# Mixer and gate weights split beside the quads of the feed-forwards and kept in DRAM; stores moved one quad later in the queue

## The chip, the cores and the metric

The kernel runs on one core of a Trainium2 chip. The metric is the device time of one execution in microseconds, lower is better. The core has a matrix engine (TensorE, PE in the profile, with its weight loads as PEld), VectorE (DVE), ScalarE (ACT), GpSimd (POOL), and SyncE (SP), which here only issues DMA transfers.

## The reference

One decoder layer on 1024 tokens of width 1024, in float32:

```
x = x + 0.5 * swiglu(rms_norm(x, ffn1_norm), ffn1_w_gu, ffn1_w_down)        # D_FF = 2816
q, k, v, u = split(rms_norm(x, mix_norm) @ w_in)                             # 512, 128, 128, 512
a = sliding_window_attention(rms_norm(q), rms_norm(k), v, rel_bias, sinks)   # window 128
m = multiscale_pool(u, pool_w, pool_scale)
x = x + concatenate([a, m]) @ w_out
x = x + 0.5 * swiglu(rms_norm(x, ffn2_norm), ffn2_w_gu, ffn2_w_down)
gate = sigmoid(rms_norm(x, ple_norm) @ ple_w_gate + ple_b_gate)
x = x + gate * rms_norm(p @ ple_w_proj, ple_post_norm)
```

## The kernel before, in words

Every large product is made of three matmuls: each float32 operand is split into a rounded part (hi, made by ScalarE) and the rest (lo, made by VectorE), and PE adds hi*hi, hi*lo and lo*hi in one bank (`three`, lines 859 to 863). Activations lie transposed, features on partitions, tokens in two halves of 512.

The program runs through six stages: the embedding projection (`e_tile`, 16 tiles copied through the buffers `et` to DRAM), the first feed-forward (phase 0), the token mixer, the second feed-forward (phase 1), and the gates.

A feed-forward is computed by a fast scheme of seven products instead of eight. Its gate and up weights come as 22 quads of 1 MB (`quad_load`). Quads 0 and 1 are computed directly (`first_product`), from quad 2 on each quad has seven products in the order P1, Q6, Q7, Q5, P2, Q4, Q3 (`product`), each of 12 matmuls. Their weight tiles live in a ring of TR = 12 slots; four of the seven are sums (`add_t`). VectorE combines the products (`quad`: w2, w3, c22, c21, c12), ScalarE copies P1 (`copy_p1`) and applies the silu to both halves (`gate0`, `gate1`). P2 adds onto P1's bank and so waits for the copy; Q3 adds onto Q5's bank and so waits for c22 (`wait_bank`, lines 948 and 963). VectorE then writes gated products (`gated`) and, after an odd quad, four mixed ones (`mix_acts`).

Beside the quads run, in SP's queue (`ffn`, lines 678 to 746): `act_store`, each second quad, of 1792 KB; for each of 22 chunks of the down weights a load (`wd_load`), four sums on POOL (`down_weights`), and a store (`wd_store`), both in the quad of the load (`wd_chunk`); and in phase 0 one piece of the embedding per quad (`e_piece`), which ScalarE squares and VectorE adds, with the sum stored after eight pieces (`e_parts`, which waits for the landing), and at quad 4 the band of relative biases. SP issues in program order and a wait holds all behind it. Then come the 77 steps of the down products (`down`), with a ring of six slots.

The mixer works through a list of steps, `PLAN`. Its weights come as 36 units of 512 KB (w_in and w_out, each column of tiles for both token halves), the gates' as 16. Each is loaded into one of two buffers raw_m, rounded by ScalarE and split by VectorE (`round_unit`, `split_unit`) into one of four slots, three units ahead of its use; the first four of a stage and the pooling weights are split during the down products. On both engines the split stands in front of what the step itself asks of them:

```
if kind in ("win", "wout") and SLOTS <= MIXU_AT[step] + LATE:
    m = MIXU_AT[step] + LATE
    if m < N_MIXU:
        split_unit(U_MIX + m)
```

Of the kernel before, what the change touches and what calls it, by code (L numbers as in the profile page):

```python
# [13 lines left out]
P = 128  # L14
# [44 lines left out]
NRAW = 2  # L59
# [6 lines left out]

LATE = SLOTS - 1
# [24 lines left out]
TR = 12  # L92
# [16 lines left out]
WD_TWO = (6, 10, 14, 17)  # L109
WD_TURN, _at = {}, 0  # L110
for _q in range(2, QUADS):
    _n = min(2 if _q in WD_TWO else 1, N_WD - _at)
    WD_TURN[_q] = tuple(range(_at, _at + _n))
    _at += _n
# [20 lines left out]
T_GAP = 1  # L135

# [66 lines left out]
def dram_unit(what, i):  # L203
# [18 lines left out]
UNIT_STEPS = [{FH + 7 + 4 * i: n for i, n in enumerate(range(U_POOLW, U_MIX + SLOTS))},  # L222
              {FH + 7 + 4 * i: n for i, n in enumerate(range(U_GATE, U_GATE + SLOTS))}]
# [38 lines left out]
def program(nc, xT, pT, units, gu, wd, poolw, small, const, onehot, rel, band_row, band, e_dram, actc, wdc, x1, out):  # L262
    with ExitStack() as ctx:
# [76 lines left out]
        raw_m = [place(f"raw_m{i}", (P, UNIT), cb + 32 * KB + 4 * KB * i) for i in range(NRAW)]  # L340
# [9 lines left out]
        def t_slot(n):  # L350
            return (n + 6) % TR
# [3 lines left out]
        t_hi = [place(f"t_hi{i}", (P, 4 * P), t_at(i) + 2 * KB, F32R) for i in range(TR)]  # L355
        ring_at = [r2, r2 + 8 * KB, t_at(10), t_at(0), t_at(2), t_at(4)]
# [104 lines left out]
        raw_in = [sem(f"raw_in{i}") for i in range(NRAW)]  # L461
        unit_hi, unit_split = sem("unit_hi"), sem("unit_split")
# [8 lines left out]
        e_out = [sem(f"e_out{i}") for i in range(4)]  # L471
# [127 lines left out]
        def _(sp):  # L599
            def unit_load(n):  # L600
                src, size = (poolw, NG * P) if n == U_POOLW else (units[mix_unit(n)], UNIT)
                if n >= NRAW:
                    sp.wait_ge(unit_split, n - NRAW + 1)
                sp.dma_start(raw_m[n % NRAW][:, 0:size], src).then_inc(raw_in[n % NRAW], 16)

# [56 lines left out]
            def e_piece(n):  # L662

                a, d = n // KT, n % KT
                if n == 0:
                    for i in range(4):
                        sp.wait_ge(e_out[i], 16 * (2 * KT // 4))
                    sp.wait_ge(s_made, made(0, "h", 1, KT - 1))
                elif d > 1:
                    sp.wait_ge(e_added, a * (KT - 1) + d - 1)  # L670
                sp.dma_start(e_part[d > 0][:, :], e_dram[a, :, d, :]).then_inc(e_back, 16)

            def e_parts(a):
                sp.wait_ge(e_added, (a + 1) * (KT - 1))
                sp.dma_start(e_dram[a, :, KT, :], e_part[0][:, :]).then_inc(e_parted, 16)
                sp.wait_ge(e_parted, 16 * (a + 1))

            def ffn(ph, first_units):
# [3 lines left out]
                for q in range(1, QUADS):  # L682
# [16 lines left out]
                    for c in WD_TURN.get(q, ()):  # L699
# [1379 lines left out]
```

## Time and profile before

| what | value |
|---|---|
| median of 3 runs | 1738.04 us (1737.92 to 1738.63) |
| the profiled execution's own time | 1737.11 us |
| its span, first to last instruction | 1735.3 us |
| mean granted TensorE clock | 0.992 |
| PE busy | 1684.5 us, 97% of the span |
| VectorE busy | 1255.8 us, 72% |
| ScalarE busy | 698.6 us, 40% |
| GpSimd busy | 233.7 us, 13% |
| DMA | 282.95 MB, mean 163 GB/s |

Busy time is the time in which an engine runs an instruction. The granted clock is a share of TensorE's full 2.4 GHz; 0.50 in a window means the lower level, 1.2 GHz, throughout it. In a timeline a row gives start and duration in us, engine, source line, operation, the tensors out<-in, and in brackets the idle time just before it and what ended it. Where the quads run, phase 0 covers about 90 to 490 us of the span, the mixer about 690 to 1005 and phase 1 from there on; the gates are the last 90 us.

### The profile page before, as it was taken

The numbers are of one execution on the slowest core, as the hardware profiler recorded it, in microseconds if no ns is written. First come the engines' busy times: TensorE is split into PE (matmuls) and PEld (weight loads), VectorE is DVE, ScalarE is ACT, GpSimd is POOL, SyncE is SP. The second block draws the span as 40 slices with busy tenths as digits, with TensorE's granted clock in tenths as the row PEclk, the third lists the DMA queues.
The fourth block names the chain that finished last, engine by engine and source line by source line (L and its number), as shares of the span: only waits on it lengthen the run. The fifth ranks groups of instructions, "written<-read, shape, count | busy, mean of one in ns | idle before, by whom it ended". The sixth has DMA issues, their size and how long they took to land.

```text
span 1735.3 us, 20459 instructions
## 1 busy us (share of the span) xinstructions
PE 1684.5 (97%) x7348; PEld 1371.6 (79%) x7348; DVE 1255.8 (72%) x1794; ACT 698.6 (40%) x1121; POOL 233.7 (13%) x245
## 2 busy tenths in 40 slices
PE   6999999999899999999999999999999999999998
PEld 4878877888788888776677788888888888888877
DVE  6888686767756768687877788777667755676785
ACT  5533232322345444356655443232223234534442
POOL 0012222222100000044140001221212300000000
PEclk9999999999999999999999999999999999999999
DMA  8135554554579765121123213454445439876533
GB/s 292 55 140 188 176 194 174 214 176 176 176 239 317 218 193 161 61 63 58 42 66 121 87 64 128 176 189 169 169 159 188 164 128 302 273 243 190 167 105 121
DMA packets 127784, 282.95 MB, mean 163 GB/s; under 512 B 10523, under 2 KB 52164, under 8 KB 119364
## 3 DMA queue, kind: packets, MB, share of 16 engines
q1 hardware_dynamic: 124376, 275.57, 47.4%
q10 hardware_dynamic: 3308, 6.08, 0.9%
q8 instruction: 59, 0.97, 0.2%
q14 instruction: 41, 0.34, 0.1%
HBM read 204.52 MB, written 78.66 MB: 163 GB/s over the span
## 4 chain that ended last, share of the span: by engine, by line
PE 61%; DMA 15%; DVE 13%; POOL 5%; ACT 4%; issue 3%; SPq 0%; ACTq 0%; DVEq 0%; POOLq 0%
PE bank L861 20%; PE bank L862 19%; PE bank L863 19%; DMA wdr<-in_wd 9%; POOL wdr L843 5%; DMA wdc<-wdr 3%; DVE qb L1902 1%; DVE hn L1521 1%; PE bank L1107 1%; ACT probs L1445 1%; DVE w_lo L1736 1%; DVE probs L1914 1%; DVE dn_lo L1728 1%; DMA e_dram<-et 1%; DMA e_dram<-e_acc 1%
## 5 line engine op out<-in xcount | busy, mean ns | idle before, releaser
L861 PE MATMUL bank<-h_hi,t_hi 128*128 128x512 f32 x704 | 274.9, 390 | 0.5 <-ACT p L1239 0.5
L862 PE MATMUL bank<-h_lo,t_hi 128*128 128x512 f32 x704 | 273.9, 389 | 0.0
L863 PE MATMUL bank<-h_hi,t_lo 128*128 128x512 f32 x704 | 273.9, 389 | 0.0
L843 POOL TENSOR_TENSOR wdr<-wdr 128x256 f32<-128x256 f32 x176 | 168.7, 959 | 748.0 <-DMA wdr<-in_wd 737.6
L1728 DVE TENSOR_TENSOR dn_lo<-d_f,dn_hi 128x1024 fp32r<-128x1024 f32 x154 | 185.1, 1221 | 116.0 <-ACT dn_hi L1256 115.7
L861 PE MATMUL bank<-dn_hi 128*128 128x512 f32 x616 | 241.1, 391 | 0.6 <-DVE dn_lo L1728 0.6
L862 PE MATMUL bank<-dn_lo,dn_hi 128*128 128x512 f32 x616 | 239.7, 389 | 0.0
L863 PE MATMUL bank<-dn_hi,dn_lo 128*128 128x512 f32 x616 | 239.7, 389 | 0.0
L861 PE MATMUL bank<-c_hi,t_hi 128*128 128x512 f32 x544 | 213.0, 392 | 10.4 <-DVE c L1600 9.0
L1256 ACT ACTIVATE dn_hi<-d_f 128x1024 fp32r<-128x1024 f32 x154 | 159.9, 1056 | 151.7 <-DMA d_f<-in_wd 78.2
L862 PE MATMUL bank<-c_lo,t_hi 128*128 128x512 f32 x544 | 212.2, 390 | 0.0
L863 PE MATMUL bank<-c_hi,t_lo 128*128 128x512 f32 x544 | 212.2, 390 | 0.0
L861 PE MATMUL bank<-h_hi,w_hi 128*128 128x512 f32 x416 | 172.1, 414 | 6.8 <-ACT sig L1485 2.6
L862 PE MATMUL bank<-h_lo,w_hi 128*128 128x512 f32 x416 | 164.0, 394 | 0.0
L863 PE MATMUL bank<-h_hi,w_lo 128*128 128x512 f32 x416 | 163.7, 394 | 0.0
L1221 ACT ACTIVATE t_hi<-t_f 128x512 fp32r<-128x512 f32 x160 | 96.0, 624 | 152.5 <-DVE t_f L1564 145.7
L861 PEld LDWEIGHTS bank<-h_hi,t_hi 128*128 128x128 f32 x704 | 132.2, 188 | 29.4 <-issue 1.4
L862 PEld LDWEIGHTS bank<-h_lo,t_hi 128*128 128x128 f32 x704 | 132.2, 188 | 27.7 <-issue 0.5
L863 PEld LDWEIGHTS bank<-h_hi,t_lo 128*128 128x128 f32 x704 | 132.2, 188 | 27.5
L861 PEld LDWEIGHTS bank<-dn_hi 128*128 128x128 f32 x616 | 115.6, 188 | 26.0 <-DVE dn_lo L1728 1.5
L862 PEld LDWEIGHTS bank<-dn_lo,dn_hi 128*128 128x128 f32 x616 | 115.7, 188 | 24.6 <-issue 0.7
L863 PEld LDWEIGHTS bank<-dn_hi,dn_lo 128*128 128x128 f32 x616 | 115.6, 188 | 24.2
(163 smaller groups left out, 2491.2 us busy)
## 6 DMA issues: line engine op xcount, KB each, us to landing
raw<-in_gu SPq DMA_DIRECT2D x44, 1024.0 KB, 6.0
d_f<-actc SPq DMA_DIRECT2D x154, 256.0 KB, 3.2
actc<-acts SPq DMA_DIRECT2D x20, 1792.0 KB, 7.8
raw_m<-in_units SPq DMA_DIRECT2D x52, 512.0 KB, 4.1
wdr<-in_wd SPq DMA_DIRECT2D x44, 512.0 KB, 5.4
wdc<-wdr SPq DMA_DIRECT2D x44, 512.0 KB, 3.4
d_f<-wdc SPq DMA_DIRECT2D x88, 256.0 KB, 3.2
d_f<-in_wd SPq DMA_DIRECT2D x66, 256.0 KB, 4.4
```

The source lines that it names most:

```text
L843: pool.tensor_tensor(blocks[to], blocks[one], blocks[two], ALU.add).then_inc(wd_made, 1)
L861: pe.matmul(ps, whi, vhi, start=first, stop=False, skip_group_check=onto)
L862: pe.matmul(ps, whi, vlo, start=False, stop=False, skip_group_check=onto)
L863: return pe.matmul(ps, wlo, vhi, start=False, stop=last, skip_group_check=onto)
L1107: last = pe.matmul(score_bank[h // 2][:, c + off:c + 2 * P], q_sb[p0:p0 + HEAD_DIM, h, b * P:(b + 1) * P], k_sb[p0:p0 + HEAD_DIM, max(b - ...
L1221: act.activation(t_hi[i][:, :], src, ACT.Copy).then_inc(t_rounded, 1)
L1256: act.activation(dn_hi[slot][:, :], d_f[slot][:, :], ACT.Copy).then_inc(dn_rounded, 1)
L1445: last = act.activation(probs[:, h, off:], probs[:, h, off:], ACT.Exp, bias=stats[:, NEGM, h:h + 1], accum_out=stats[:, DEN, h:h + 1])
L1521: dve.scalar_tensor_tensor(hn[k % 2][:, :], x_sb[:, k, tok(nrm % 2)], col(g), rstd[nrm % 2][:, :], ALU.mult, ALU.mult).then_inc(h_normed, 1)
L1728: dve.tensor_tensor(dn_lo[slot][:, :], d_f[slot][:, :], plain(dn_hi[slot][:, :]), ALU.subtract).then_inc(dn_split, 1)
L1736: dve.tensor_tensor(lo, raw_m[n % NRAW][:, 0:size], plain(hi), ALU.subtract).then_inc(unit_split, 1)
L1902: link(dve.reciprocal(qb[j % 2][:, :], qb[j % 2][:, :]))
```

## The change

The units are split once each, not once for each token half: 10 of w_in, 8 of w_out (phase 0, quads 2 to 19) and 8 of the gate (phase 1, quads 2 to 9). Each quad loads one unit, rounds and splits it, and stores both parts to a new DRAM tensor hl (26 units of 1 MB) one quad later. The mixer and the gates load the finished parts, two DMAs of 512 KB for each of the 52 uses, straight into the four slots; ScalarE and VectorE no longer touch them. The unit's buffers take two slots of the tile ring, so TR is 10. In SP's queue the stores of tiles, sums and units stand one quad after their loads. The head copies with eight et buffers and in another order, the first norm's sum stands after tile 4 instead of 2, and quad 3's first sums move ahead of quad 2.

```
-WD_TWO = (6, 10, 14, 17)
+WD_TWO = (7, 13)
-for _q in range(2, QUADS):
+for _q in range(1, QUADS - 1):
...
-TR = 12
+TR = 10
+NET = 8
+U_QUAD = 2
+N_SPLIT = N_IN + 2 * KT
+SPLITS = [list(range(N_IN + KT)), list(range(N_IN + KT, N_SPLIT))]
...
+        def unit_ready(n):
+            return w_in[(n - U_MIX) % SLOTS], 32 * ((n - U_MIX) // SLOTS + 1)
...
             def unit_load(n):
...
+                if slot_free(n):
+                    sp.wait_ge(main_made, slot_free(n))
+                else:
+                    sp.wait_ge(gu_made, NGU if n < U_GATE else 2 * NGU)
+                    sp.wait_ge(unit_out, 32 * (len(SPLITS[0]) if n < U_GATE else N_SPLIT))
+                s = (n - U_MIX) % SLOTS
+                sp.dma_start(plain(w_hi[s][:, :]), hl[mix_unit(n) - W_IN][:, 0:UNIT]).then_inc(w_in[s], 16)
+                sp.dma_start(plain(w_lo[s][:, :]), hl[mix_unit(n) - W_IN][:, UNIT:2 * UNIT]).then_inc(w_in[s], 16)
+
+            def split_load(u):
+                if u:
+                    sp.wait_ge(unit_out, 32 * u)
+                sp.dma_start(unit_f[:, :], units[W_IN + u]).then_inc(unit_in, 16)
+
+            def split_store(u):
+                sp.wait_ge(unit_lo, u + 1)
+                sp.dma_start(hl[u][:, 0:UNIT], plain(unit_rounded[:, :])).then_inc(unit_out, 16)
+                sp.dma_start(hl[u][:, UNIT:2 * UNIT], plain(unit_low[:, :])).then_inc(unit_out, 16)
...
             def e_parts(a):
...
-                sp.wait_ge(e_parted, 16 * (a + 1))
...
-                    if ph == 0 and 0 <= q - E_QUAD <= 2 * KT:
-                        n = q - E_QUAD
-                        if n and n % KT == 0:
-                            e_parts(n // KT - 1)
-                        if n < 2 * KT:
-                            e_piece(n)
+                    if 0 < q - U_QUAD <= len(SPLITS[ph]):
+                        split_store(SPLITS[ph][q - U_QUAD - 1])
                     if q % 2 == 0:
                         act_store(ph, q // 2 - 1)
+                    if q - 1 in WD_TURN:
+                        wd_store(ph, WD_TURN[q - 1][-1])
+                    n = q - E_QUAD
+                    if ph == 0 and n in (KT, 2 * KT):
+                        e_parts(n // KT - 1)
+                    if q in WD_TURN:
+                        wd_load(ph, WD_TURN[q][0])
+                    if ph == 0 and 0 <= n < 2 * KT:
+                        e_piece(n)
+                    if 0 <= q - U_QUAD < len(SPLITS[ph]):
+                        split_load(SPLITS[ph][q - U_QUAD])
                     if ph == 0 and q == BAND_QUAD:
...
-                    for c in WD_TURN.get(q, ()):
-                        wd_chunk(ph, c)
...
                         quad_load(ph, q + 3)
+                    for a, b in zip(WD_TURN.get(q, ()), WD_TURN.get(q, ())[1:]):
+                        wd_store(ph, a)
+                        wd_load(ph, b)
...
                     gate0(ph, q)
-                    gate1(ph, q)
                     if ph == 0 and 0 <= q - E_QUAD < 2 * KT:
                         e_squares(q - E_QUAD)
+                    if 0 <= q - U_QUAD < len(SPLITS[ph]):
+                        round_unit(SPLITS[ph][q - U_QUAD])
+                    gate1(ph, q)
...
                 make_c21(ph, q)
+                if ph == 0 and 0 <= q - E_QUAD < 2 * KT:
+                    e_accumulate(q - E_QUAD)
+                if 0 <= q - U_QUAD < len(SPLITS[ph]):
+                    split_unit(SPLITS[ph][q - U_QUAD])
                 make_c12(ph, q)
...
-                if kind in ("win", "wout") and SLOTS <= MIXU_AT[step] + LATE:
-                    m = MIXU_AT[step] + LATE
-                    if m < N_MIXU:
-                        round_unit(U_MIX + m)
...
             round_pj(0)
-            round_pj(1)
             act.wait_ge(small_in, 16)
-            for k in range(KH):
-                x_square(0, k)
             for n in range(2 * KT):
                 e_tile(n)
-                if n < 2:
...
+                if n == 0:
+                    x_square(0, 0)
+                    x_square(0, 1)
+                    round_pj(1)
+                elif n < 4:
+                    x_square(0, 2 * n)
+                    x_square(0, 2 * n + 1)
+                elif n == 4:
                     std(0)
```

## Rows read from the trace of the kernel before

**Rows 1.** PE's waits: who ended them, us in total, times, longest.

```profile
PE bank L861 <- DVE pj_lo L1849: 9.4, 1, 9.4
PE bank L861 <- DVE c L1600: 9.0, 5, 5.0
PE bank L861 <- DVE probsT_lo L1875: 6.6, 3, 4.3
PE bank L1118 <- DVE probs L1927: 6.3, 5, 2.4
PE bank L861 <- ACT et L1360: 4.7, 3, 2.6
PE bank L861 <- ACT sig L1485: 2.6, 2, 1.3
PE bank L861 <- DVE h_lo L1527: 2.6, 1, 2.6
```

**Rows 2.** Windows: us, busy (instructions) of PE, PEld, DVE, ACT, POOL, PEclk, DMA share, GB/s.

```profile
440.00:444.00 4.00, 4.00 (x12) 3.14 (x12) 2.57 (x5) 0.63 (x1) 0.00 (x0) 0.63 0.93 360
764.00:768.00 4.00, 4.00 (x14) 2.93 (x14) 1.92 (x2) 1.96 (x4) 0.00 (x0) 0.60 0.51 152
824.00:828.00 4.00, 4.00 (x8) 2.12 (x7) 2.87 (x12) 0.80 (x4) 0.00 (x0) 0.50 0.12 50
957.00:961.00 4.00, 3.65 (x11) 2.88 (x12) 1.15 (x3) 1.49 (x2) 0.00 (x0) 0.67 0.11 40
```

**Rows 3.** Timeline of ACT and PE around quads 2 and 3, both phases.

```profile
1069.60 0.60 ACT L1239 ACTIVATE p<-bank 128x512 f32<-128x512 f32 x1 [3.40 <-PE bank L863]
...
1088.64 0.60 ACT L1239 ACTIVATE p<-bank 128x512 f32<-128x512 f32 x1 [4.08 <-PE bank L863]
...
104.76 0.47 PE L861 MATMUL bank<-c_hi,t_hi 128*128 128x512 f32 x1 [1.41 <-DVE t_lo L1576]
```

**Rows 4.** Chain of waits (start, us, what), phase 0, and SP's timeline, phase 1.

```profile
107.58 7.60 DMA wdr<-in_wd
...
119.88 3.40 DMA wdc<-wdr
...
123.30 6.53 DMA wdr<-in_wd
...
137.72 18.46 DMA wdr<-in_wd
...
1062.55 0.33 SPq L625 DMA_DIRECT2D actc<-acts  x1
```

**Rows 5.** Splits of units and VectorE's mixed sums: by tile, by form, timeline.

```profile
L1736 DVE TENSOR_TENSOR w_lo<-raw_m,w_hi x52: 1207/1220/2078, 535.8 to 1711.1; 128x1024 fp32r<-128x1024 f32 x52
...
L1263 ACT ACTIVATE w_hi<-raw_m 128x1024 fp32r<-128x1024 f32 x28 | 29.3, 1046 | 4.2 <-DMA raw_m<-in_units 4.2
...
104.57 2.61 DVE L1643 TENSOR_TENSOR acts<-acts 128x512 f32<-128x512 f32 x4
```

**Rows 6.** Timeline of ACT and PE in phase 0.

```profile
213.06 0.63 ACT L1231 ACTIVATE e_part<-e_part 128x512 f32<-128x512 f32 x1 [11.45 <-DMA e_part<-e_dram]
...
222.22 0.47 PE L861 MATMUL bank<-c_hi,t_hi 128*128 128x512 f32 x1 [2.20 <-DVE c L1600]
...
439.71 0.77 PE L861 MATMUL bank<-c_hi,t_hi 128*128 128x512 f32 x1 [5.05 <-DVE c L1600]
```

**Rows 7.** Timeline of PE and ACT in the mixer.

```profile
764.00 0.79 PE L861 MATMUL bank<-h_hi,w_hi 128*128 128x512 f32 x1 [2.57 <-DVE h_lo L1527]
...
820.48 1.09 PE L1118 MATMUL bank<-const_sb,probs 128*128 128x128 f32 x8 [2.40 <-DVE probs L1927]
...
957.35 0.50 PE L861 MATMUL bank<-probsT_hi,v_hi 128*128 128x512 f32 x1 [4.29 <-DVE probsT_lo L1875]
...
950.96 1.06 ACT L1263 ACTIVATE w_hi<-raw_m 128x1024 fp32r<-128x1024 f32 x1 [4.25 <-DMA raw_m<-in_units]
```

**Rows 8.** Timeline of PE at the first feed-forward product.

```profile
42.30 0.50 PE L861 MATMUL bank<-h_hi,t_hi 128*128 128x512 f32 x1
```

More of the change, by code:

```diff
@@ L58 @@
 W_GATE = W_OUT + KT
-NRAW = 2
 N_MIXU = 2 * N_IN + 2 * KT
@@ L218 @@
 assert N_WIN0 % 2 == 0 and N_GATE0 % 2 == 0
-UNIT_STEPS = [{FH + 7 + 4 * i: n for i, n in enumerate(range(U_POOLW, U_MIX + SLOTS))},
-              {FH + 7 + 4 * i: n for i, n in enumerate(range(U_GATE, U_GATE + SLOTS))}]
+POOLW_STEP = FH + 7
+U_QUAD = 2
+N_SPLIT = N_IN + 2 * KT
+SPLITS = [list(range(N_IN + KT)), list(range(N_IN + KT, N_SPLIT))]
 def unit_of(step):
@@ L259, with program @@
 H_AT = {2: 0, 3: 1, 6: 2, 7: 3}
-def program(nc, xT, pT, units, gu, wd, poolw, small, const, onehot, rel, band_row, band, e_dram, actc, wdc, x1, out):
+def program(nc, xT, pT, units, gu, wd, poolw, small, const, onehot, rel, band_row, band, hl, e_dram, actc, wdc, x1, out):
     with ExitStack() as ctx:
@@ L339, in program @@
         w_lo = [place(f"w_lo{i}", (P, UNIT), cb + 8 * KB * i + 4 * KB, F32R) for i in range(SLOTS)]
-        raw_m = [place(f"raw_m{i}", (P, UNIT), cb + 32 * KB + 4 * KB * i) for i in range(NRAW)]
+        raw_m = place("raw_m", (P, NG * P), cb + 32 * KB)
         sq = [place(f"sq{i}", (P, HALF), cb + 40 * KB + 2 * KB * i) for i in (0, 1)]
@@ L355, in program @@
         t_hi = [place(f"t_hi{i}", (P, 4 * P), t_at(i) + 2 * KB, F32R) for i in range(TR)]
+        unit_f = place("unit_f", (P, UNIT), t_at(TR + 1))
+        unit_rounded = place("unit_rounded", (P, UNIT), t_at(TR), F32R)
+        unit_low = place("unit_low", (P, UNIT), t_at(TR + 1), F32R)
         ring_at = [r2, r2 + 8 * KB, t_at(10), t_at(0), t_at(2), t_at(4)]
@@ L398, in program @@
         pj_lo = [place(f"pj_lo{i}", (P, UNIT), t_at(t_slot(FIRST + i)), F32R) for i in (0, 1)]
-        et = [place(f"et{i}", (P, HALF), cb + 2 * KB * i) for i in range(4)]
+        et = [place(f"et{i}", (P, HALF), cb + 2 * KB * i) for i in range(NET)]
         gband = place("gband", (N_Q_HEADS, SKEW), cb + 24 * KB)
-        oh_sb = place("oh_sb", (N_BUCKETS + 1, SKEW), t_at(t_slot(FIRST + 2)))
+        oh_sb = place("oh_sb", (N_BUCKETS + 1, SKEW), t_at(TR))
         e_part = [place("e_acc", (P, HALF), acc_at[1]), place("e_part", (P, HALF), rstd_at[1])]
@@ L460, in program @@
         x1_out = [sem(f"x1_out{a}") for a in (0, 1)]
-        raw_in = [sem(f"raw_in{i}") for i in range(NRAW)]
-        unit_hi, unit_split = sem("unit_hi"), sem("unit_split")
+        poolw_in, poolw_hi, poolw_split = sem("poolw_in"), sem("poolw_hi"), sem("poolw_split")
+        unit_in, unit_hi, unit_lo, unit_out = sem("unit_in"), sem("unit_hi"), sem("unit_lo"), sem("unit_out")
+        w_in = [sem(f"w_in{i}") for i in range(SLOTS)]
         pj_in, pj_rounded, pj_split = [sem(f"pj_in{i}") for i in (0, 1)], sem("pj_rounded"), sem("pj_split")
@@ L470, in program @@
         e_copied = sem("e_copied")
-        e_out = [sem(f"e_out{i}") for i in range(4)]
+        e_out = [sem(f"e_out{i}") for i in range(NET)]
         re_out = [sem(f"re_out{a}") for a in (0, 1)]
@@ L665, in e_piece @@
                 if n == 0:
-                    for i in range(4):
-                        sp.wait_ge(e_out[i], 16 * (2 * KT // 4))
+                    for i in range(NET):
+                        sp.wait_ge(e_out[i], 16 * (2 * KT // NET))
                     sp.wait_ge(s_made, made(0, "h", 1, KT - 1))
+                elif d == 0:
+                    sp.wait_ge(e_parted, 16)
                 elif d > 1:
@@ L737, in ffn @@
                         else:
-                            for j in range(4):
-                                sp.wait_ge(e_out[j], 16 * (2 * KT // 4))
+                            for j in range(NET):
+                                sp.wait_ge(e_out[j], 16 * (2 * KT // NET))
                             for a in (0, 1):
@@ L1198, in round_s @@
                     act.wait_ge(gu_made, ph * NGU + FIRST)
-                elif what == ("s", Q5, 0) and ph == 0:
-                    for i in range(4):
-                        act.wait_ge(e_out[i], 16 * (2 * KT // 4))
+                elif what == ("h", 1, 0) and ph == 0:
+                    for i in range(NET):
+                        act.wait_ge(e_out[i], 16 * (2 * KT // NET))
                 act.activation(operand("hi", what), source(what), ACT.Copy).then_inc(s_rounded, 1)
@@ L1693, in quad @@
                 todo = [(q + 1, s) for s in LOS1] if more else []
-                if ph == 0 and 0 <= q - E_QUAD - 1 < 2 * KT:
-                    e_accumulate(q - E_QUAD - 1)
                 if q == 2:
                     split_t(ph, *todo[0])
-                if more:
+                elif more:
                     add_t(ph, q + 1, 0)
@@ L1708, in quad @@
                 make_w3(ph, q)
-                for x in todo[1:3]:
+                for x in todo[1 + (q == 2):3]:
                     split_t(ph, *x)
@@ L1991, in build @@
     x1 = nc.dram_tensor("x1", (D_MODEL, SEQ), F32, kind="Internal").ap()
-    program(nc, xT, pT, units, gu, wd, poolw, small, const, onehot, rel, band_row, band, e_dram, actc, wdc, x1, out)
+    program(nc, xT, pT, units, gu, wd, poolw, small, const, onehot, rel, band_row, band, hl, e_dram, actc, wdc, x1, out)
 def constants():
```

115 lines of the change are left out of this document (52 added, 63 removed).

## The prediction

> **What bounds the kernel now.** Read first the shares of the page: PE is busy 1684.5 of 1735.3 us, and no matmul is added or taken away, so the change can only move PE's 50.8 us of idle time and the time at the lower clock. The list of PE's waits splits the idle time [rows 1]: 9.4 us before the first matmul, 4.7 for the copies of the embedding tiles (et), 9.0 for the sums of the quads (c), 15.5 in the mixer (probsT_lo, probs, h_lo), 2.6 in the gates (sig). The windows [rows 2] show what a gap costs beyond itself: after gaps of over 2.3 us the clock stood at 0.50 to 0.67, the lower of the two levels for most of 4 us, so 1.3 to 2.0 us of work lost each; behind 824:828 a part of the windows before is lost as well, and over the whole mixer I count 8.2 us so, from its windows' clock. The gap before 439.71 [rows 6] cost another 1.5 to 1.7.
>
> **The clock of a quad.** p1 is copied at 1069.60 and 1088.64 [rows 3]: a quad takes 19.04 us, one of its seven products 2.72. In its order P1, Q6, Q7, Q5, P2, Q4, Q3, the product P2 starts 10.9 us into the quad and needs the p1 copy; Q3 starts at 16.3 and needs c22. VectorE's instructions on 128x512 follow each other every 0.65 us (2.61 for four, [rows 5]). A split on 128x1024 is 1.05 on ScalarE and 1.22 on VectorE, at worst 2.08 [rows 5]; I take 1.05 and 1.3.
>
> **What the queue now carries.** Each split stands before gate1 on ScalarE and before c12 on VectorE. If the unit is not there, everything behind waits: gate1 and the next quad's p1 copy on ScalarE; c12, two gated products, (after an odd quad) four mixed ones, the next quad's four sums, splits, w2, w3 and c22 on VectorE. From the end of the split to that c22 are 13 instructions (8.5 us), 17 (11.1 us) after an odd quad. So PE stalls once a split ends later than 7.8 us (even quad) or 5.2 us (odd) into the next quad. The load of the unit is issued last: behind the store of the unit before (two transfers of 512 KB), the store of the sums (1792 KB, each second quad), the store of the tiles, and the tiles' load, which waits until that store has landed. Price of these waits [rows 4]: sums and a 512 KB tile issued together land after 7.60 us from the second issue, 8.0 from the first; a lone 512 KB store takes 3.40, a load with others before it 6.53. I take 6.1 for tiles, embedding piece and unit together (1280 KB; between 3.4 and 7.6 by the rows), and 6.2 for unit store plus tile store.
> - Odd quad, split to split: 6.2 + 6.1 + 1.05 + 1.3 + some 1 us of issue and overlap with POOL = 15.7.
> - Even quad: 4.7 (c12, gated, mixed) + 8.0 + 6.1 + 2.35 + 1 = 22.2.
> Together 37.9 against 38.1 for PE's two quads: just balanced, an odd quad recovers what an even one loses. In this steady part I cost the change at 0 to 2 us; the cover is gone once a pair of quads needs more (rival below).
>
> The Trainium skill, GPSIMD Engine Reference, section Specifications, says that GpSimd and VectorE share their SBUF interfaces when a VectorE instruction has two inputs there. The split's 2.08 beside its 1.22 [rows 5] agrees; 26 splits that all met the tile sums would take 22 us more of VectorE. The Trainium skill, DMA: Bandwidth & Descriptors, section Anatomy of one DMA, gives about 2.0 us plus bytes over 436 GB/s: 5.0 us for the 1280 KB where I took 6.1, and 7.4 where the trace has 8.0; by it the two first-unit stalls below would each be 1 us shorter.
>
> **Part by part.**
> 1. *First unit, phase 0.* In quad 2 nothing has been fetched ahead. The store of the sums is issued 0.4 us before 107.58 [rows 4]; the tile store, now ready by then, takes the place of the load that landed 7.60 later: about 116.3 with 1 us for VectorE slowed by the tile sums. Then 6.1: 122.4. Split done 124.7, c22 of quad 3 at 133.2. Quad 2's last product starts at 104.76 [rows 3], so quad 3 at 107.48 and its Q3 at 123.8: a stall of 9.4, of which 6.3 fall already at P2 (copy ready 124.7, wanted 118.4). I take 8.5, since parts of VectorE's chain overlap, plus 1.5 of clock: +10. Bounds +5 to +13.
> 2. *Phase 1, the same place.* VectorE and SP run as in phase 0, shifted by 955.3 (1062.55 against 107.2, [rows 4]); PE's quad 3 starts at 1066.9 [rows 3], shifted by 959.4. So 4.1 us more cover, and no embedding piece (0.8): stall 3.5 to 4.5, clock 1: +5. Bounds 0 to +8.
> 3. *The band* is sent at quad 4 behind the unit. In 137.72's row [rows 4] a tile waited 18.46 us behind sums, weights and band; at the 2304 KB per 8.0 us of the pair about 11 of it are the others, 8 the band. It now delays quad 5's unit store, so its split ends some 10.5 us into quad 6: 5.3 over the limit, with clock +6. Bounds 0 to +10.
> 4. *Two tiles in quads 7 and 13.* The second one's sums are stored only in the next quad, behind POOL (4.6 us of sums between 115.26 and 119.88, [rows 4]) and before the tile load: lag 10.5 against 7.8, twice: +5. Bounds 0 to +8.
> 5. *What goes.* SP no longer waits within a quad for POOL, nor for the embedding sum's landing. That wait held ScalarE 11.45 us at 213.06 and PE 2.20 at 222.22, and 5.05 at 439.71 [rows 6]. All of c's 9.0, 0.5 for the copy, 1.7 clock: -11. Bounds -4 to -11. Late next are the units of 1, 3 and 4.
> 6. *Head.* Eight et buffers and the copies ahead of the squares take away the 4.7 us for et [rows 1] and the slow clock behind it. The first norm now stands after tile 4, behind all eight squares, and gives back about 2, as the reciprocal comes 1 us later. The first gate product, now at 42.30 [rows 8], starts 3 us sooner: -3. Bounds 0 to -6.
> 7. *Mixer.* 28 splits leave each of both engines between 726 and 1006: 29.3 us of ScalarE and 28 times 1.22 or more of VectorE [rows 5]. The gap at 764.00 (2.57) ends VectorE's alternating of norm tiles and splits; the one at 957.35 (4.29) follows a ScalarE wait of 4.25 for a unit queued behind the next phase's weights [rows 7]. Both lose 2.5 to 3. Before 820.48 a split stands ahead of the scores: 1.2 of 2.40 [rows 7]. In sum I count 13 of the 15.5 plus 1.5 for smaller waits as going, 6.5 of the 8.2 of clock, and 3 coming back since PE catches up with the reciprocals: -17. Bounds -6 and -23. A slot's 1 MB has three units of 24 matmuls (16 us) to arrive, 8.0 us by the pair: 0.
> 8. *Gates:* 12 splits less; sig's 2.6 [rows 1] mostly goes: -2. Bounds 0 to -3.
> 9. *Ten t slots for twelve, reordered sums of quad 3, fewer splits in the down products:* 0; the fourth sum now waits for Q7, for which w3 behind it waits anyway, and PE shows no wait in the down products. Uncovered, the slots would cost one product, 2.7.
>
> Sum: 10 + 5 + 6 + 5 - 11 - 3 - 17 - 2 = -7, against this execution's 1737.1 us: 1730. The median of the runs shown is 0.9 higher; I say 1731.
>
> **Rivals.**
> - *The SP round trip becomes the bound (slower).* If DMA under the added 1.5 MB per quad, or POOL beside VectorE, makes a pair of quads take 40.5 instead of 37.9, each pair from quad 4 on costs 2.4: seven pairs 17, and 4 of clock. It decides from 38.1 on, 0.2 above my sum. For it: the tile behind mixed traffic took 6.53 although its bytes alone need half. Against: the pair landed 2304 KB in 8.0 us, 288 KB per us, and by the sizes of the transfers two quads now carry about 9.3 MB in 38 us, 245 KB per us. Time 1731 + 21 = 1752, with half the drift 1742.
> - *The stalls 1 to 4 hardly show,* as VectorE and the products have more slack than I read; then only 5 to 8 act with a third of the 26: 1738 - 33 + 9 = 1714. For it: phase 1 before has no quad stall. Against: the 5.05 at 439.71 shows that late sums do reach PE.
> - *The mixer's gaps are the chain scores, exp, probs itself,* and removed splits only turn into VectorE idle time: gain 7 instead of 17: 1741. For it: probs alone holds 6.3 us of PE's waits [rows 1]. Against: 957.35.
>
> **Chances.** My sum 0.40 (own range 1724 to 1738), SP bound 0.27, no stalls 0.18, mixer chain 0.15. About 0.2%, 3.5 us, is what a measurement here tells from no change. Faster: 0.30 of the first, all of the third: and 0.03 of the rest, 0.51. Same: 0.07 of the first, 0.05 of the second, 0.06 of the last: 0.18. Slower: the rest, 0.31. The range runs from near the stall-free case to most of the SP case: 1714 to 1752.
>
> **What would show it.** PE waits for p1 or c at quad 3 of both phases, ScalarE's split there waiting for DMA over 8 us; another at quads 6, 8 and 14; no PE wait over 3 us in the mixer; clock near 1.0 there. Wrong would be a first-unit stall under 4 us, or waits for c in every second quad.

## The result, and the profile after

The changed kernel takes 1716.28 us (median of 3 runs, 1715.31 to 1719.83) against 1738.04: ratio 0.9879, 95% interval 0.9856 to 0.9901. The prediction was 1731, range 1714 to 1752: 7 us faster forecast, 21.8 measured. The direction and the range held, the size did not: 1716.3 lies at the fast end of the range of 1714 to 1752, and outside the 1724 to 1738 that the prediction gave its own sum.

Each profiled execution is cut at PE's first matmul of each kind of work; the lengths of the stages show where the time went (us):

| stage | before | after | difference | predicted |
|---|---|---|---|---|
| head, to the first gate product | 42.30 | 40.97 | -1.3 | -3 |
| quads, phase 0 | 439.85 | 442.58 | +2.7 | +10 (parts 1, 3, 4, 5) |
| down products, phase 0 | 212.89 | 212.71 | -0.2 | 0 |
| mixer | 308.17 | 281.29 | -26.9 | -17 |
| quads, phase 1 | 425.23 | 432.37 | +7.1 | +5 |
| down products, phase 1 | 210.83 | 210.81 | 0.0 | 0 |
| gates | 96.03 | 92.77 | -3.3 | -2 |

PE's waits after (who ended them, us in total, times, longest), to be laid beside [rows 1]:

```profile
PE bank L889 <- ACT p L1268: 10.2, 2, 6.4
...
PE bank L889 <- DVE c L1629: 4.3, 3, 1.9
PE bank L917 <- DVE acc L1538: 2.0, 1, 2.0
PE bank L889 <- ACT et L1392: 1.6, 2, 1.0
...
PE bank L1146 <- DVE probs L1961: 1.0, 1, 1.0
```

probsT_lo, h_lo and sig are gone from the list, probs fell from 6.3 to 1.0, c from 9.0 to 4.3. New is p, ScalarE's copy of P1, with 10.2 in two waits; both stand in quad 3, behind the first unit of a phase. The gap before acc, 2.0 where it was 0.7, is what the head gives back.

The five new or remaining gaps of the quads after, besides the 1.4 of quad 2 that was there before (timeline of PE; start, duration, in brackets the idle time before it and what ended it):

```profile
123.66 0.77 PE L889 MATMUL bank<-h_hi,t_hi 128*128 128x512 f32 x1 [6.40 <-ACT p L1268]
...
191.18 0.47 PE L889 MATMUL bank<-c_hi,t_hi 128*128 128x512 f32 x1 [1.65 <-DVE c L1629]
...
250.65 0.47 PE L889 MATMUL bank<-c_hi,t_hi 128*128 128x512 f32 x1 [1.89 <-DVE c L1629]
...
365.95 0.47 PE L889 MATMUL bank<-c_hi,t_hi 128*128 128x512 f32 x1 [0.78 <-DVE c L1629]
...
1055.89 0.77 PE L889 MATMUL bank<-h_hi,t_hi 128*128 128x512 f32 x1 [3.83 <-ACT p L1268]
```

How the first comes about is read from SP's timeline and then ScalarE's, the counterpart of [rows 4]:

```profile
107.71 0.33 SPq L647 DMA_DIRECT2D actc<-acts  x1
108.08 0.59 SPq L643 DMA_DIRECT2D wdc<-wdr  x1
114.77 0.58 SPq L639 DMA_DIRECT2D wdr<-in_wd  x1
115.67 0.33 SPq L693 DMA_DIRECT2D e_acc<-e_dram  x1
116.05 0.42 SPq L621 DMA_DIRECT2D unit_f<-in_units  x1
...
119.50 0.63 ACT L1260 ACTIVATE e_acc<-e_acc 128x512 f32<-128x512 f32 x1 [15.90 <-DMA e_acc<-e_dram]
121.45 1.06 ACT L1289 ACTIVATE unit_rounded<-unit_f 128x1024 fp32r<-128x1024 f32 x1 [1.33 <-DMA unit_f<-in_units]
122.42 0.61 ACT L1277 ACTIVATE w<-w 128x512 f32<-128x512 f32 x1
122.94 0.58 ACT L1268 ACTIVATE p<-bank 128x512 f32<-128x512 f32 x1
```

SP stands from 108.7 to 114.8 for the tile store to land; only then does it issue the tile, the embedding piece and the unit. ScalarE waits 15.90 us for the piece, then 1.33 more for the unit, and the copy of p, which has to wait behind both and behind gate1, comes 6.4 us late for PE.

The clock behind the two long gaps (windows of 4 us; us, busy time and instructions of PE, PEld, DVE, ACT and POOL, granted clock, DMA share, GB/s):

```profile
124.00:128.00 4.00, 4.00 (x10) 3.10 (x10) 3.78 (x7) 0.66 (x2) 0.00 (x0) 0.50 0.85 335
128.00:132.00 4.00, 4.00 (x15) 3.01 (x13) 4.00 (x8) 3.20 (x6) 0.00 (x0) 0.78 0.49 154
...
1056.00:1060.00 4.00, 4.00 (x10) 3.17 (x11) 3.78 (x8) 0.77 (x2) 0.59 (x1) 0.50 0.79 313
1060.00:1064.00 4.00, 4.00 (x16) 3.10 (x14) 4.00 (x8) 3.33 (x7) 0.00 (x0) 0.80 0.52 159
...
192.00:196.00 4.00, 4.00 (x19) 3.31 (x18) 2.04 (x4) 0.00 (x0) 0.00 (x0) 1.00 0.65 189
```

Two windows at 0.50 and 0.78 are 2.0 + 0.9 us of work lost, at 0.50 and 0.80 2.0 + 0.8. In this profile the clock stays at 1.00 behind the gap of 1.65 at 191.18, and behind 1.89 and 0.78 too. Such costs do not repeat from one execution to the next, as the last section shows.

The mixer as one window, before and then after:

```profile
695.00:1003.20 308.20, 290.98 (x1259) 226.99 (x1259) 232.49 (x438) 159.28 (x326) 64.80 (x65) 0.97 0.24 75
```

```profile
696.30:977.50 281.20, 279.94 (x1259) 222.93 (x1258) 192.93 (x406) 129.82 (x294) 58.66 (x65) 1.00 0.44 145
```

The same 1259 matmuls: PE's idle time falls from 17.2 to 1.3 us, its busy time from 291.0 to 279.9, by 11.0. The granted clock explains 8.4 of the 11.0: so much do PE's busy time and the missing share of the clock give, multiplied and summed over windows of 0.5 us, and after the change the clock is 1.00 throughout. The other 2.6 are matmuls that took longer at a granted clock of 1.00. VectorE is busy 39.6 us less, ScalarE 29.5 less.

### The profile page after: what moved, and what is told of

Its sections match the earlier page's. It is cut to its first block and busy times, and to the rows that moved or that the text cites. A ratio compares the mean times of both kernels' runs of the same rounds, so it can differ in the third digit from the quotient of the medians.

```text
span 1713.5 us, 20509 instructions
## 1 busy us (share of the span) xinstructions
PE 1678.1 (98%) x7348; PEld 1371.2 (80%) x7348; DVE 1196.9 (70%) x1768; ACT 677.1 (40%) x1095; POOL 227.2 (13%) x245
## 5 line engine op out<-in xcount | busy, mean ns | idle before, releaser
L889 PE MATMUL bank<-h_hi,t_hi 128*128 128x512 f32 x704 | 277.0, 393 | 10.2 <-ACT p L1268 10.2
L1763 DVE TENSOR_TENSOR dn_lo<-d_f,dn_hi 128x1024 fp32r<-128x1024 f32 x154 | 184.9, 1220 | 125.0 <-ACT dn_hi L1285 124.7
L889 PEld LDWEIGHTS bank<-h_hi,t_hi 128*128 128x128 f32 x704 | 133.2, 189 | 39.9 <-issue 11.5
```

Source lines behind the costliest of these rows:

```text
L889: pe.matmul(ps, whi, vhi, start=first, stop=False, skip_group_check=onto)
L1763: dve.tensor_tensor(dn_lo[slot][:, :], d_f[slot][:, :], plain(dn_hi[slot][:, :]), ALU.subtract).then_inc(dn_split, 1)
```

## The experiments

The kernel before was timed anew beside each group of runs, and its median was 1738.6 to 1740.9 there; so ratios are compared rather than medians. The stage lengths are those of the profiled executions. Where the code of a stage is the same they repeat to 0.1 us in the mixer and to 2 us in the quads of phase 0. Theory A and rival B are those of the expectation that stands above each reading.

| run | median | ratio, 95% interval | quads 0 | mixer | quads 1 |
|---|---|---|---|---|---|
| changed kernel | 1716.28 | 0.9879 (0.9856 to 0.9901) | 442.58 | 281.29 | 432.37 |
| e1_early | 1712.26 | 0.984 (0.9821 to 0.9859) | 441.66 | 281.32 | 430.49 |
| e2_unit_first | 1698.11 | 0.9757 (0.9741 to 0.9773) | 433.80 | 281.36 | 426.96 |
| e9_two_early | 1693.26 | 0.9737 (0.9719 to 0.9754) | 427.88 | 281.38 | 425.22 |
| e12_tile_first | 1702.38 | 0.9786 (0.9773 to 0.9798) | 435.52 | 281.39 | 425.23 |
| e5_queue_only | 1731.79 | 0.9951 (0.9937 to 0.9965) | 430.20 | 309.39 | 425.23 |
| e7_band1 | 1714.95 | 0.9854 (0.9841 to 0.9868) | 442.49 | 281.39 | 432.67 |
| e11_two_moved | 1720.69 | 0.989 (0.9872 to 0.9909) | 446.64 | 281.33 | 432.66 |
| e6_heavier | 1725.2 | 0.9916 (0.9904 to 0.9929) | 449.43 | 281.38 | 432.64 |
| e8_net4 | 1716.76 | 0.9867 (0.9854 to 0.9879) | 443.25 | 281.39 | 432.53 |
| e3_mix_dve | 1732.32 | 0.9961 (0.9947 to 0.9974) | 441.82 | 297.38 | 432.11 |
| e4_mix_act | 1718.08 | 0.9878 (0.9857 to 0.99) | 442.14 | 283.72 | 432.89 |
| e10_mix_both | 1736.64 | 0.9989 (0.9977 to 1.0001) | 443.61 | 302.49 | 432.33 |

### The mixer: e3_mix_dve, e4_mix_act, e10_mix_both

e3 adds this to VectorE's loop over the steps of the mixer:

```
             for step in PLAN:
                 kind = step[0]
+                if kind in ("win", "wout") and SLOTS <= MIXU_AT[step] + 3 < N_MIXU:
...
+                    dve.tensor_tensor(pad_d[:, :], pad_d[:, :], pad_d[:, :], ALU.subtract).then_inc(pad_dve, 1)
```

e4 adds the same to ScalarE's loop, with a copy, and e10 adds both:

```
+                    act.activation(pad_a[:, :], pad_a[:, :], ACT.Copy).then_inc(pad_act, 1)
```

> The changed kernel with 28 padding subtractions on 128x1024 put back on VectorE in the mixer, at the steps where the splits of the kernel before stood (in place on an unused region; they wait for nothing else). It computes the same. Theory A (VectorE's time was what held PE in the mixer, 13 of the 15.5 us of waits through VectorE): most of the 26.9 us that the mixer gained is given back, 15 to 20: 1732 to 1736, with PE waits for probs, h_lo and probsT_lo as in the kernel before. Rival B (the splits held PE by what they waited for, the rounding on ScalarE and a unit behind other transfers, not by their time): under 6 us: 1722 or less.

> The changed kernel with 28 padding copies on 128x1024 put back on ScalarE in the mixer, at the steps where the roundings stood, VectorE without its padding. It computes the same. Theory A: ScalarE was busy for half of the mixer only (159 of 308 us), so its 29.3 us cost PE little: 0 to 5 us, 1716 to 1721. Rival B (ScalarE holds probsT and the copies at the end of the chain of scores, exp, probs): 8 us or more, 1724.

> The changed kernel with both paddings. Theory A: the engines' time is nearly all: the sum of the two alone plus 1 to 3 us, 20 us or more over the changed kernel, about 1737; what is then missing of 26.9 is what the late unit at 957.35 cost (4.3 of wait and its 2 of clock). Rival B: far under 20 us; the rest, over 10 us, was waiting for data, not engine time.

The list has 32 such steps, not 28: the row with 28 in [rows 5] begins at 726, and four stand before it. VectorE's padding alone, 233.5 - 192.9 = 40.6 us of its time, gives back 16.1 us of the mixer's 26.9, and 0.8% of the 1.2% by the ratios. ScalarE's padding alone lengthens the mixer by 2.4 us, which does not show in the ratio. Both together give back 21.2 us, and the gain as a whole is gone but for 0.1% (the interval reaches 1.0001). Theory A holds in all three. Of the 2.6 us of longer matmuls at full clock 2.0 are back under e3, which adds nothing but VectorE's work; so they go with the waits for VectorE, though how is not shown. PE's gaps under e3 (timeline of PE):

```profile
781.04 0.66 PE L1149 MATMUL bank<-const_sb,probs 128*128 128x128 f32 x4 [1.82 <-DVE probs L1972]
817.50 1.09 PE L1149 MATMUL bank<-const_sb,probs 128*128 128x128 f32 x8 [2.40 <-DVE probs L1972]
...
947.92 0.50 PE L892 MATMUL bank<-probsT_hi,v_hi 128*128 128x512 f32 x1 [0.45 <-DVE probsT_lo L1916]
```

The 2.40 is the gap of 820.48 in [rows 7], now with a subtraction that waits for nothing: VectorE's time makes it. The gap of 957.35 in [rows 7] (4.29) comes back only as 0.45. The padding waits for no unit, so that gap was the late unit; with the slow clock behind it (957:961 at 0.67, [rows 2]) it is 3.8 + 1.3 = 5.1 of the 5.7 us that both paddings leave open (308.2 - 302.5).

### The first units: e1_early

```
                     if q + 3 < QUADS:
                         ...
                         quad_load(ph, q + 3)
+                    if q == 1:
+                        if ph == 0:
+                            e_piece(0)
+                        split_load(SPLITS[ph][0])
```

(both left out in quad 2)

> The changed kernel, with the first unit of each phase (and the first embedding piece) loaded one quad earlier, at quad 1, where the DMA queues stand idle. Theory A (the first unit's load, queued behind the sums and the first tile, is the whole of the wait at quad 3): the waits 6.40 (phase 0) and 3.83 (phase 1) for p go, and with them 2.9 and 2.8 us of slow clock: 1716.3 - 15.9 = 1700.4. Rival B (SyncE's chain of loads and stores is bound by itself, the first unit only sets where it starts): what goes at quad 3 comes back as waits for c in the quads behind, over 5 us of them per phase; 1708 or more.

Rival B, in the main. Both waits at quad 3 are gone, but phase 0's quads are only 0.9 us shorter and phase 1's 1.9. The waits for c behind them come to 8.3 us in phase 0; in phase 1 there is one of 3.37, less than the 5 that B named. The time, 1712.3, is B's. Timeline of PE under e1:

```profile
137.86 0.47 PE L893 MATMUL bank<-h_hi,t_hi 128*128 128x512 f32 x1 [2.21 <-ACT p L1272]
148.93 0.76 PE L893 MATMUL bank<-c_hi,t_hi 128*128 128x512 f32 x1 [5.35 <-DVE c L1633]
191.10 0.47 PE L893 MATMUL bank<-c_hi,t_hi 128*128 128x512 f32 x1 [1.24 <-DVE c L1633]
250.37 0.47 PE L893 MATMUL bank<-c_hi,t_hi 128*128 128x512 f32 x1 [1.73 <-DVE c L1633]
```

And the reason, from SP's timeline of the same run:

```profile
107.50 0.59 SPq L643 DMA_DIRECT2D wdc<-wdr  x1
114.17 0.57 SPq L639 DMA_DIRECT2D wdr<-in_wd  x1
...
115.44 0.43 SPq L625 DMA_DIRECT2D hl<-unit_rounded  x1
...
122.75 0.55 SPq L643 DMA_DIRECT2D wdc<-wdr  x1
128.43 0.57 SPq L639 DMA_DIRECT2D wdr<-in_wd  x1
...
129.69 0.43 SPq L621 DMA_DIRECT2D unit_f<-in_units  x1
```

The first unit was split by 111.2, but its store stood behind SP's wait for the tile store and went at 115.44, and the next unit's load behind the next tile store at 129.69. The lateness belongs to SP's row of waits, not to one transfer.

### The order in the queue: e2_unit_first, e9_two_early, e12_tile_first

e2 is e1 with the tile's load moved behind embedding piece and unit in every quad:

```
-                    if q in WD_TURN:
-                        wd_load(ph, WD_TURN[q][0])
                     if ph == 0 and 0 < n < 2 * KT:
                         e_piece(n)
                     if 0 < q - U_QUAD < len(SPLITS[ph]):
                         split_load(SPLITS[ph][q - U_QUAD])
+                    if q in WD_TURN:
+                        wd_load(ph, WD_TURN[q][0])
```

> As e1_early, and in every quad the embedding piece and the unit are sent ahead of the wait for the tile store, the tile behind them. Theory A (what is left of the waits for c in phase 0, 4.3 us at 191, 251 and 366, is the unit coming behind the tile): they go too, 1700.4 - 5 = 1695. Rival B (they come from VectorE's own load of work in those quads, or from POOL's sums, which now come later): the same as e1_early within 2 us, or up to 4 us more, with new waits behind POOL.

Theory A, and more than it said: ratio 0.9757, 14 us below e1 where 5 were expected. The waits at 191 and 250 are gone, and those behind the second unit shrank too, from 2.21 and 5.35 to 3.98 in phase 0 and from 3.37 to 1.45 in phase 1. One gap of 3.98 at 145.17 is left in phase 0 and 1.45 at 1069.10 in phase 1. e9 sends unit 0's store within quad 2 and unit 1's load at the end of it:

```
+                    if q == U_QUAD:
+                        split_store(SPLITS[ph][0])
                     if q in WD_TURN:
                         wd_load(ph, WD_TURN[q][0])
                     ...
-                    if q == 1:
+                    if q in (1, 2):
                         if ph == 0:
-                            e_piece(0)
-                        split_load(SPLITS[ph][0])
+                            e_piece(q - 1)
+                        split_load(SPLITS[ph][q - 1])
```

> As e2_unit_first; besides, unit 0 is stored within quad 2, ahead of that quad's tile load, and unit 1 (in phase 0 the second embedding piece too) is loaded at the end of quad 2 instead of in quad 3. Theory A (the wait of 3.98 for c at 145.17 and of 1.45 in phase 1 are the second unit, whose load at 124.61 waited for a store issued 4 us after the split had ended): both go, with some 2 us of clock: 1698 - 7 = 1691. Rival B (the lateness moves to the next quad again, as it did from quad 3 to quad 4 when the first unit came early): 1696 or more, with a wait for c at quad 5.

Theory A: 1693.26 us, ratio 0.9737, the best kernel here, 1.4% below the changed one. Its interval (0.9719 to 0.9754) overlaps that of e2 (0.9741 to 0.9773); the trace decides, since both of e2's waits are gone from it. Phase 1's quads are back at the length they have with no unit to split (425.22 against 425.23). All that PE still waits for in the quads of both phases, from its list of waits:

```profile
PE bank L895 <- DVE t_lo L1611: 1.4, 1, 1.4
...
PE bank L895 <- DVE c L1635: 0.6, 1, 0.6
```

The 1.4 was there before (1.41 at 104.76, [rows 3]). e12 keeps e9's start and puts the tile ahead of the unit again from quad 3 on.

> As e9_two_early (units 0 and 1 fetched ahead), but from quad 3 on the tile goes ahead of the embedding piece and the unit again, as in the changed kernel. Theory A (the prediction's balance of the loop, 37.9 us for a pair of quads against PE's 38.1, holds; only the start, the band and the two doubled tiles make it late): at most three waits for c, near quads 6, 9 and 15, 2 to 5 us in all; 1693 + 4 = 1697. Rival B (a loop with the tile ahead of the unit is too slow by itself): waits for c in every second quad, over 10 us; 1704 or more.

Between the two. By the waits it is A: two for c, in quads 6 and 15, 5.3 us in all, and none in phase 1, so the loop as changed does not drift. By the time, 1702.4, it is nearer to B's 1704 than to A's 1697. The wait behind the band is 4.28, with 2.8 of clock (0.50 and 0.76 in the two windows of 4 us from 184 on), where e9 has 0.57, so the order is worth 9 us here, more than the 4 expected. Timeline of PE under e12:

```profile
184.41 0.77 PE L895 MATMUL bank<-c_hi,t_hi 128*128 128x512 f32 x1 [4.28 <-DVE c L1635]
359.63 0.47 PE L895 MATMUL bank<-c_hi,t_hi 128*128 128x512 f32 x1 [1.00 <-DVE c L1635]
```

### The terms of the loop: e7_band1, e11_two_moved, e6_heavier

`BAND_QUAD = 4` becomes 1; `WD_TWO = (7, 13)` becomes `(10, 16)`; and for e6, with 48 in place of 32 in the waits for `unit_out`:

```
                 sp.dma_start(hl[u][:, UNIT:2 * UNIT], plain(unit_low[:, :])).then_inc(unit_out, 16)
+                sp.dma_start(more[u], plain(unit_low[:, :])).then_inc(unit_out, 16)
```

> The changed kernel with the band sent at quad 1 instead of quad 4. Theory A (part 3 of the prediction: the band delays the units behind it): the wait of 1.65 us for c at 191.18 goes, 1714.5. Rival B (that wait is what is left of the late first unit, which takes until quad 6 to be caught up): it stays at 1 us or more; 1716. A band that delays the first tile or the first unit instead would show as a longer wait than 6.40 at quad 3: 1718 or more.

The gap at 191.18 went, as A says, but so did those at 250.65 and 365.95, and in their place stands one wait of 11.76 at quad 3 (and 1.32 after it):

```profile
129.11 0.77 PE L889 MATMUL bank<-h_hi,t_hi 128*128 128x512 f32 x1 [11.76 <-ACT p L1268]
137.59 0.47 PE L889 MATMUL bank<-c_hi,t_hi 128*128 128x512 f32 x1 [1.32 <-DVE c L1629]
```

The longer wait at quad 3 is what the expectation named as a band that delays the first tile or unit, though not at its 1718 us: the time is 1714.95, and the stage is as long as in the changed kernel, 442.49 against 442.58. In quad 3 the waits are 6.7 us longer and the clock costs 1.4 us less (windows of 0.5 us: 1.6 against 3.0); that took the place of 4.3 us of waits in quads 6, 9 and 15. The likely reading is that once PE has been set back far enough, later delays of the queue fit into what it has lost already: the waits of one queue are not a sum of terms, PE pays for the latest point. It rests on this run and on e1.

> The changed kernel with the doubled tiles in quads 10 and 16 instead of 7 and 13. Theory A (part 4 of the prediction: the second tile delays the next unit): the waits for c at 250.65 (1.89) and 365.95 (0.78) go from there and stand three quads later, near 308 and 423; 1716 as before. Rival B (they are what was left of the late start): they stay at 250 and 366, 1716 too.

Theory A: the two gaps now stand three quads later. The time did not stay at 1716: the median is 1720.7 and the quads of phase 0 take 4.1 us more, though the ratios' intervals overlap. Of this 2.3 us are the gap at 427.37, which is 3.11 where the one at 365.95 was 0.78; the rest lies about as far as such runs differ.

```profile
309.72 0.47 PE L889 MATMUL bank<-c_hi,t_hi 128*128 128x512 f32 x1 [1.11 <-DVE c L1629]
...
427.37 0.47 PE L889 MATMUL bank<-c_hi,t_hi 128*128 128x512 f32 x1 [3.11 <-DVE c L1629]
```

> The changed kernel with a third store of 512 KB for every unit (the low half once more, to a place of its own that nothing reads), for which the next load waits as for the other two. Theory A (the loop has 0.2 us to spare for a pair of quads, so nearly every us that is added to it reaches PE): at the 288 KB per us of the prediction 1.8 us per quad, 3.4 per pair after the spare; eight pairs of phase 0 and three of phase 1: 30 to 40 us, 1746 to 1756. Rival B (the loop has more slack than reckoned, or the third store lies beside the others): under 10 us, 1726 or less.

Rival B: 0.4% over the changed kernel by the ratios, 9 us by the medians, 7 by the quads of phase 0 and 0.3 in phase 1. The waits for c still stand in quads 3, 6, 9 and 15 and not in every second quad (0.48, 4.45, 2.19 and 0.66). How much room there was is read from ScalarE's roundings of the units of quads 4, 5, 7, 8, 9, 10 and 11, first after (timeline of ScalarE):

```profile
156.65 1.06 ACT L1289 ACTIVATE unit_rounded<-unit_f 128x1024 fp32r<-128x1024 f32 x1 [1.27 <-DMA unit_f<-in_units]
177.91 1.06 ACT L1289 ACTIVATE unit_rounded<-unit_f 128x1024 fp32r<-128x1024 f32 x1 [2.00 <-DMA unit_f<-in_units]
...
213.79 1.06 ACT L1289 ACTIVATE unit_rounded<-unit_f 128x1024 fp32r<-128x1024 f32 x1 [0.86 <-DMA unit_f<-in_units]
239.97 1.06 ACT L1289 ACTIVATE unit_rounded<-unit_f 128x1024 fp32r<-128x1024 f32 x1 [1.54 <-DMA unit_f<-in_units]
255.81 1.06 ACT L1289 ACTIVATE unit_rounded<-unit_f 128x1024 fp32r<-128x1024 f32 x1 [1.14 <-DMA unit_f<-in_units]
277.34 1.06 ACT L1289 ACTIVATE unit_rounded<-unit_f 128x1024 fp32r<-128x1024 f32 x1 [2.00 <-DMA unit_f<-in_units]
291.20 1.06 ACT L1289 ACTIVATE unit_rounded<-unit_f 128x1024 fp32r<-128x1024 f32 x1 [0.79 <-DMA unit_f<-in_units]
```

and under e6, quads 9 and 11:

```profile
260.18 1.06 ACT L1290 ACTIVATE unit_rounded<-unit_f 128x1024 fp32r<-128x1024 f32 x1 [1.09 <-DMA unit_f<-in_units]
...
297.58 1.07 ACT L1290 ACTIVATE unit_rounded<-unit_f 128x1024 fp32r<-128x1024 f32 x1 [1.41 <-DMA unit_f<-in_units]
```

Each of them waits for its unit, so the queue sets the pace while it catches up. After, from quad 9 to quad 11: 21.5 + 13.9 = 35.4 us for the pair, 2.7 under PE's 38.1. With the band the step into an odd quad is 21.3 instead of 13.9 (156.65 to 177.91), with a doubled tile the step into an even one 26.2 instead of 21.5 (213.79 to 239.97): 7.4 and 4.7 us. With the third store the pair takes 37.4: the 512 KB cost 1.0 us per quad, not 1.8, and the loop is still 0.7 under. Both figures rest on this one pair of quads.

### The queue's part alone: e5_queue_only, and the head: e8_net4

e5 is the kernel before with the new WD_TURN and WD_TWO and the new places of `wd_load`, `wd_store`, `e_parts` and `e_piece`, as in the diff above; no unit is split beside the quads.

> The kernel before with only the queue part of the change: tiles stored one quad later, two tiles in quads 7 and 13, no wait of SyncE for the embedding sum's landing; units split in the mixer as before, twelve t slots, head as before. Theory A (prediction, part 5): c's 9.0 us of waits in phase 0, 0.5 for the copy and 1.7 of clock go: 1738 - 11 = 1727, the sound range 1727 to 1734. Rival B (these waits are VectorE's own, met by POOL's sums beside it): less than 4 us, 1734 or more.

Theory A: phase 0's quads fall from 439.85 to 430.20, 9.7 us, and the medians differ by 9. No wait for c is left, but one of 2.31 for p at quad 3 is new: the first tile store is waited for there also without a unit, and ScalarE's copy of p stands behind the embedding piece (8.26 us of waiting for it, until 121.84).

> The changed kernel with four buffers for the embedding tiles of the head instead of eight. Theory A (part 6 of the prediction: the buffers take away the waits for et): waits for et rise from 1.6 by 2 us or more, 1719. Rival B (the new order of squares and copies does it alone): 1 us or less, 1717.

Between the two: the waits for et rise by 1.3 us, from 1.6 to 2.9, the head from 40.97 to 42.10, and the times cannot be told apart. So the buffers are worth about 1 us, and the new order does the rest.

## Why the prediction was off in size

The mechanisms were largely right; what failed is the size of parts 3, 4 and 7. Phase 0's quads came out 7.3 us below the forecast, the mixer 9.9 and the gates 1.3, while the head and phase 1's quads gave 3.8 us less than forecast: 14.7 us in all. That the range of 1714 to 1752 still held is owed to the rivals that it took in. By its own parts:

1. *First unit, phase 0* (+10): right. It had the unit landing at 122.4 (by 121.45), the split done at 124.7 (123.8), c22 at 133.2 (132.0), and 6.3 of the wait at P2 (6.40). The 3.1 at Q3 did not come: PE ran at the lower clock in between, so its loss of 2.9 there and the rest of the delay covered each other. 9.3 in all. In e3, e4 and e10, with the same quads, 0.6 to 1.2 of it did come.
2. *First unit, phase 1* (+5): 3.83 + 2.8 = 6.6, the stage says 7.1. The wait was right, the clock 1 where it was 2.8.
3. and 4. *Band and doubled tiles* (+6 and +5): the places were right within one quad (6, 9, 15), e11 shows the second; the size was 4.3 in all, with no clock. The band's own delay was sized well (8 for 7.4), and so was the limit: the split of quad 5's unit ended 7.0 us into quad 6 (180.2, Q3 being wanted at 189.5), against a limit of 5.5 by the 10.8 us that VectorE's 17 instructions took, and 1.65 of wait followed. The mis-sized term is the loop: 13.9 us into an odd quad and 21.5 into an even one, not 15.7 and 22.2. It had 2.7 us to spare in a pair of quads, not 0.2, so late units were caught up, and this split came at 7.0 and not at 10.5. Adding stalls was a mistake besides, as e7 suggests.
5. *What goes* (-11): right. 9.0 + 0.5 + 1.7 = 11.2 is what closes the stage's account: 9.3 + 4.3 - 11.2 = 2.4 against 2.7 measured. e5 alone shows 9.7, with its own 2.31.
6. *Head* (-3): -1.3 in this pair of profiles, which is not like with like. Behind the 2.0 us before acc the clock fell in some profiles of the new head (40.67 to 41.21, the changed kernel's 40.97 among them) and not in others (40.22 to 40.43). The old head has 42.30 without such a spell and 43.99, in e5, with one. Like with like the new head gives 2 to 3 us. The eight buffers are about 1 of it (e8), the order the rest.
7. *Mixer* (-17): -26.9, the largest miss. The attribution held: VectorE's time, and one late unit. Three sizes failed, beside the count of splits. Waits: 14.5 were counted as going, and 16.0 went. Clock: 6.5 of 8.2 were counted as going, and all 8.4 went. The 3 us that were to come back, PE catching up with the reciprocals, did not: probs holds 1.0. The 2.6 us of longer matmuls at full clock were no term of the sum. (The parts as given there add up to 18, not 17.) The low bound of -23 was too narrow too.
8. *Gates* (-2): -3.3, just outside its bound of -3.

The prediction's rule for the clock, the lower level behind gaps of over 2.3 us, does not hold in the trace that it was read from: behind the gap of 1.82 at 785.67 the clock fell as well and cost 1.7 us. So the clock terms of parts 1, 2 and 5 came out as they did partly by luck.

Of the signs that it named, the waits at quad 3 of both phases, a mixer with no wait over 3 us and a clock of 1.00 there came true; the further waits stood at quads 6, 9 and 15 for 6, 8 and 14. A first-unit stall under 4 us was to count as wrong: phase 1's is 3.83, within the 3.5 to 4.5 of its own part 2, so that sign did not fit the prediction's own bounds.

Of the rivals, the SP round trip as the bound, given 0.27, is refuted by e12 and e6: there is no drift. The mixer chain (0.15) is refuted by e3: the removed splits turned into PE's time by four tenths (16.1 us for 40.6 us of VectorE). "The stalls hardly show" (0.18, 1714) came nearest in time, but for a reason that was not its own: the stalls did show, some 20 us of them with their clock, and the mixer's 26.9 us paid for them.

On the pages: the Trainium skill, GPSIMD Engine Reference, section Specifications, has VectorE and GpSimd share their SBUF interfaces. This trace agrees: splits of 1.51, 1.60 and 1.70 us had GpSimd busy for 1.43 to 1.62 of them, and splits with GpSimd idle took 1.22. But the 26 splits beside the quads took 1314 ns in the mean and 1225 in the median, so it cost them 2.3 us in all, not the 22 of the worst case. The Trainium skill, DMA: Bandwidth & Descriptors, section Anatomy of one DMA, gives its 2.0 us plus bytes over 436 GB/s for a DMA that GpSimd issues, while these are issued by SyncE, so the prediction borrowed it. It would have the 1280 KB ahead of the first split take 5.0 us (an estimate by its figures); from the issue of the unit to its landing this trace has 5.4, from the issue of the tile, the first of the three, 6.7. The 6.1 taken from rows was the nearer.

## What to carry to other kernels

- When a queue of issues with waits is made to carry one more round trip, first ask at which point it starts empty-handed. Here the steady loop was fine, and 16 of the 20 us that the stalls cost with their clock lay behind the first unit of each phase; sending two transfers into the idle queue ahead of them, and the transfer that engines wait for ahead of the one that nobody does, was worth as much again as the change itself (1716 to 1693).
- Delays in one queue need not add up: here PE paid for the latest point, and a loop with 7% to spare gave back the rest. Sum the lag, not the stalls.
- Moving work from a stage where an engine stands before PE in a chain to one where it has room can pay well below the engine's time (here 16 us for 41), and part of the pay is the matrix engine's clock behind the gaps (here 8 of 27 us). Count both, the clock from the granted clock in short windows: PE's busy time over the same matmuls held another 2.6 us that were not clock.
- Before a difference of 1 or 2 us between two profiles is explained, look whether a gap that both have was followed by the lower clock in only one of them.

## What the runs showed of the hardware

- The length of a gap does not tell what it costs by the clock. The gap of 2.0 us before acc in the head stands in the profiles of all twelve kernels with the new head: in six of them (the changed kernel, e6, e7, e8, e11 and e12) the clock fell with it, at a cost of 1.7 us, and in the other six it did not. The gap of 2.40 before probs cost 3.4 in the kernel before ([rows 7] and the window 824:828 of [rows 2]) and nothing in e3, e5 and e10. The 3.11 at 427.37 in e11 cost nothing, and behind 1.82 at 785.67 before the clock fell. Windows behind the gap before acc in the changed kernel, then in e1:

```profile
22.50:26.50 4.00, 3.94 (x10) 2.84 (x11) 3.83 (x3) 2.11 (x4) 0.00 (x0) 0.68 1.00 306
```

```profile
22.50:26.50 4.00, 3.79 (x15) 2.83 (x16) 3.83 (x4) 2.79 (x4) 0.00 (x0) 1.00 0.97 314
```

- All 23 gaps from 3.37 us up in the quads and the mixers of the fourteen traces stood beside a spell of the lower clock, and the loss did not grow with the gap. By windows of 0.5 us it was 1.4 to 2.9 us for gaps of 3.37 to 4.47, 3.0 for the 6.40 and 1.6 for the 11.76 of e7.
- Of the mixer's 26.9 us 8.4 were clock, as the windows of the kernel before had shown (8.2 by the prediction's count). PE's busy time fell by more, 11.0.
- 26 further stores of 512 KB, 13.6 MB in all, cost 9 us, though the queue waits for each of them to land. One of them added 1.0 us to a round; a lone store of that size took 3.40 ([rows 4]). So most of their time lay beside transfers that were under way already.
